# A chunked recurrence in a token mixer: its small matrices as two heads by four chunks of 64x64, on diagonal quarters of the TensorE array

## The chip, the cores and the metric

The kernel runs on one core of a Trainium2 chip. The metric is the device time of one execution in microseconds, as the median of several runs. An engine is one of TensorE (PE in the profile; its weight loads are PEld), VectorE (DVE), ScalarE (ACT), GpSimd (POOL) and SyncE (SP, which here only issues transfers).

## The reference: what is computed

Two transformer blocks on 256 tokens of width 1024, all in fp32. The first block is a SwiGLU feed-forward, a token mixer and another feed-forward, each on a normalised input and added to the residual. The second has two kinds of attention, a dense feed-forward and a mixture of eight experts. Only the token mixer is touched. It projects the input to 3344 columns and splits them in four branches of 256 channels:

```python
y_pool = causal_multiscale_pool(p_pool, ...)                    # windows 2, 4, 8, 16, then a small linear map
o_h    = chunked_gated_linear_attention(q, k, v, log_f)         # 4 heads of 64, "hgrn"
S_t    = S_{t-1} diag(w_t) - (S_{t-1} kk_t)(kk_t * a_t)^T + v_t k_t^T ;  o_t = S_t r_t    # "rwkv", 4 heads of 64
o_g    = chunked_gated_linear_attention(q, k, v, log_a)         # 4 heads of 64, "gla"
y      = concatenate([y_pool, y_hgrn, y_rwkv, y_gla]) ; return y @ w_out
```

The change is about the third branch, the rwkv recurrence over 256 steps, and about the order of the work of the other branches around it.

## The kernel before

**Lanes.** The program is written as one list of steps for each engine (`Lane`); a step waits for the marks given to it and leaves one. The order on an engine is the order in which the Python code emits the steps. Small helpers emit them: `MM` a product (one fp32 product is two instructions in the trace, each with its own weight load), `TT`, `TS`, `STT` elementwise work on VectorE or GpSimd, `AC` an operation of ScalarE. In the trace all steps of a helper have the helper's line, so L1189 is any product of the mixer. ScalarE changes its function table when an operation needs another set of functions; that is an instruction of its own in the trace, ACT_TABLE_LOAD. PSUM has eight banks of 512 columns (`bank[0..7]`).

**Input product.** `linear` multiplies 13 chunks of weights (`MIX_ORDER`) and calls `between` twice for each chunk. Every call advances two generators one step, `left()` (the gla attention, then the preparation `rwkv()`) and `hgrn()` (the hgrn attention). So their work lies between the chunks on each engine. What is left of them is run off behind the last chunk by `zip_longest(*streams)`. `rwkv()` waits there until the last chunk (`held[0]`) is there, then does the small products for decay, rate and gate (L1189 `sb_lora`), with tanh and sigmoid, the square root of the head sums, and a scan over the decays.

**Preparation.** Behind that stands elementwise work on VectorE that makes decayed keys, queries and values (`kkd`, `rd`, `kp`, `bp`, `kc`, `bc_`), and transposes by `to_tokens` (L1196) with copies by ScalarE. `qr` is an operand padded with zeros: four copies spread two heads over it, so that one full 128-row product gives both heads. All this waits for the end of the first attention (`own["done"]`), and the recurrence's products wait for the last copies (`pe.wait(m_kct, m_bct, m_tok, m_g)`).

**Recurrence.** Four heads are two tiles (`ti`) of two heads. The time is cut in four chunks of 64 steps (`RCHUNK`). Inside a chunk the recurrence is a triangular system. `tile_stages(ti)` keeps its matrices as four full 128x128 ones (`probs`: two heads by two blocks of two chunks), of which only the two diagonal 64x64 blocks are not zero. It has these parts, between `yield`s:

- Masks: for each block three score products into `ba`, `bb_`, `bc_`, and seven VectorE operations with 128x128 masks (`akt`, `abt`, `xx`, `invt`, `inv`, `art`, `arbt`).
- Inverse by doubling: for w in 2, 4, 8, 16, 32 a product (`mx`), its copy by ScalarE (`xx`), products with the inverse and its transpose (`mb_`, `ma`), and two additions on VectorE; GpSimd masks the next level's matrix (`ml`).
- Solve: products with the solved values `yy`, then outputs and chunk states in 64x64 products, then a chain over the chunks 1 and 2 and the last products, which end in `outs[ti]`.

`others()` is a third generator: the pool branch (`bands`, `wp`), the norm and gate of the hgrn branch (output part 1) and of the gla branch (output part 3), and the split of each finished branch into a high and a low part (`split`). `zip_longest(tile_stages(0), tile_stages(1), others())` takes the three in turns; that fixes the order on every engine.

**End.** The group mean (a product with `headsum`) starts when both tiles and the gla branch are through. Then `project` multiplies the four branches by `w_out` in the order 0, 1, 3, 2, with `group_norm()` between, whose result is branch 2 and is used last. `ahead` and `fetch` emit the transfer of a weight chunk (SyncE, line 257) and its split into a high part (ScalarE, L263) and a low part (VectorE, L267). The next phase, the second feed-forward, needs the whole result.

## Time and profile before

| | us |
|---|---|
| median of 3 runs | 1711.46 |
| lowest and highest of them | 1709.71 and 1711.62 |
| the profiled execution | 1713.05 |
| its span in the trace | 1711.2 |
| TensorE busy | 1615.1 |
| VectorE busy | 1216.3 |
| ScalarE busy | 871.7 |
| GpSimd busy | 128.2 |

All rows are of the one profiled execution, and times are microseconds from the start of its span. Busy time is what the profiler recorded; matmuls overlap, so their mean duration is longer than their distance. A timeline row gives the start of the first instruction of a merged run, the time to the end of its last one, their count and, in brackets, how long the engine had been idle and what released it. The stage that the change rewrites runs from the end of the input product (330.4) to the group mean (418.07).

### The profile page before, as it was taken

Reading aid. Unit: us, or ns where it says so; the run is one execution under the profiler, and the core shown is the slowest. Engines: PE = TensorE matmul, PEld = TensorE weight load, DVE = VectorE, ACT = ScalarE, POOL = GpSimd, SP = SyncE. Lnnn points to the kernel's source line nnn. Section 1 sums busy time; section 2 is a strip of 40 time slices with the busy share of each in tenths; the row PEclk is TensorE's granted clock in tenths of the full one; section 3 lists DMA queues with packets and bytes.
Section 4 is the critical chain, followed back from the end, with each engine's and each line's share of the span. In section 5 each row is a group of like instructions: output and inputs, shape, how many; then the busy total and the mean of one; then the engine's idle time right before and its main releaser. Section 6 shows DMA issues by size and latency. Waiting matters only on the chain.

```text
span 1711.2 us, 23833 instructions
## 1 busy us (share of the span) xinstructions
PE 1615.1 (94%) x9812; PEld 1391.3 (81%) x9812; DVE 1216.3 (71%) x1447; ACT 871.7 (51%) x1011; POOL 128.2 (7%) x142
## 2 busy tenths in 40 slices
PE   7999989888999998989899999889999999999997
PEld 6999979777899998946799987568877877877875
DVE  5777769754677775444677763557888988988996
ACT  5334456442533344343434342447777777777775
POOL 1000012310000000052000001520000000000000
PEclk9999999989999998999899999998999999999999
DMA  8777633210588764504577760025998988988983
GB/s 307 282 282 263 235 120 130 85 50 26 199 334 300 289 236 146 175 25 162 197 276 264 265 241 1 1 99 225 367 329 315 363 320 309 367 322 325 347 322 131
DMA packets 51918, 386.45 MB, mean 226 GB/s; under 512 B 5888, under 2 KB 6224, under 8 KB 7904
## 3 DMA queue, kind: packets, MB, share of 16 engines
q1 hardware_dynamic: 50400, 376.16, 59.9%
q0 software_dynamic: 1408, 8.73, 1.3%
q8 instruction: 80, 1.31, 0.3%
q14 instruction: 30, 0.25, 0.0%
HBM read 383.82 MB, written 1.05 MB: 225 GB/s over the span
## 4 chain that ended last, share of the span: by engine, by line
PE 79%; DVE 9%; ACT 5%; issue 3%; DMA 2%; POOL 2%; DVEq 0%; ACTq 0%; SPq 0%
PE bank L295 21%; PE bank L297 21%; PE bank L296 20%; PE bank L1189 5%; PE bank L455 2%; DVE sb_wlo L267 2%; ACT sb_whi L263 2%; DMA sb_ada_raw<-in_ada 1%; PE bank L1755 1%; PE bank L1714 1%; DVE sb_ada_acc L600 1%; DVE sb_wlo L2181 1%; PE bank L1910 1%; PE bank L1870 1%; PE bank L610 1%
## 5 line engine op out<-in xcount | busy, mean ns | idle before, releaser
L267 DVE TENSOR_TENSOR sb_wlo<-sb_raw,sb_whi 128x2048 fp32r<-128x2048 f32 x137 | 313.7, 2291 | 191.4 <-ACT sb_whi L263 191.4
L295 PE MATMUL bank<-sb_xhi,sb_whi 128*128 128x256 f32 x1344 | 384.3, 286 | 6.6 <-DVE sb_wlo L267 6.1
L296 PE MATMUL bank<-sb_xlo,sb_whi 128*128 128x256 f32 x1344 | 382.1, 284 | 0.0
L297 PE MATMUL bank<-sb_xhi,sb_wlo 128*128 128x256 f32 x1344 | 382.0, 284 | 0.0
L263 ACT ACTIVATE sb_whi<-sb_raw 128x2048 fp32r<-128x2048 f32 x137 | 261.5, 1909 | 183.6 <-PE bank L297 178.6
L295 PEld LDWEIGHTS bank<-sb_xhi,sb_whi 128*128 128x128 f32 x1344 | 259.7, 193 | 10.7 <-DVE sb_wlo L267 7.0
L296 PEld LDWEIGHTS bank<-sb_xlo,sb_whi 128*128 128x128 f32 x1344 | 259.9, 193 | 1.1
L297 PEld LDWEIGHTS bank<-sb_xhi,sb_wlo 128*128 128x128 f32 x1344 | 259.7, 193 | 0.0
L2181 DVE TENSOR_TENSOR sb_wlo<-sb_raw,sb_whi 128x2048 fp32r<-128x2048 f32 x84 | 191.5, 2286 | 16.2 <-ACT sb_whi L2175 14.6
L295 PE MATMUL bank<-sb_whi,sb_slots_hi 128*128 128x512 f32 x448 | 182.4, 407 | 0.0
L297 PE MATMUL bank<-sb_whi,sb_slots_lo 128*128 128x512 f32 x448 | 176.7, 394 | 0.0
L296 PE MATMUL bank<-sb_wlo,sb_slots_hi 128*128 128x512 f32 x448 | 176.6, 394 | 0.0
L2175 ACT ACTIVATE sb_whi<-sb_raw 128x2048 fp32r<-128x2048 f32 x84 | 160.8, 1916 | 26.9 <-PE bank L297 26.5
L295 PE MATMUL bank<-sb_whi,sb_hhi 128*128 128x512 f32 x368 | 146.4, 398 | 1.1 <-DVE sb_hlo L574 1.1
L297 PE MATMUL bank<-sb_whi,sb_hlo 128*128 128x512 f32 x368 | 144.9, 394 | 0.0
L296 PE MATMUL bank<-sb_wlo,sb_hhi 128*128 128x512 f32 x368 | 144.8, 393 | 0.0
L600 DVE SCALAR_TENSOR_TENSOR sb_ada_acc<-sb_ada_raw,sb_cact,sb_ada_acc 128x384 f32<-128x384 f32 x224 | 138.6, 619 | 6.9
L297 PEld LDWEIGHTS bank<-sb_whi,sb_slots_lo 128*128 128x128 f32 x448 | 84.1, 188 | 20.1
L296 PEld LDWEIGHTS bank<-sb_wlo,sb_slots_hi 128*128 128x128 f32 x448 | 84.6, 189 | 16.5
L295 PEld LDWEIGHTS bank<-sb_whi,sb_slots_hi 128*128 128x128 f32 x448 | 84.3, 188 | 16.4
L295 PEld LDWEIGHTS bank<-sb_whi,sb_hhi 128*128 128x128 f32 x368 | 69.9, 190 | 15.8 <-issue 1.2
L297 PEld LDWEIGHTS bank<-sb_whi,sb_hlo 128*128 128x128 f32 x368 | 69.7, 189 | 15.3
(465 smaller groups left out, 2574.4 us busy)
## 6 DMA issues: line engine op xcount, KB each, us to landing
sb_raw<-in_ffn SPq DMA_DIRECT2D x98, 1024.0 KB, 4.8
sb_raw<-in_moe SPq DMA_DIRECT2D x86, 1024.0 KB, 5.0
sb_ada_raw<-in_ada SPq DMA_DIRECT2D x32, 1536.0 KB, 6.5
sb_cst<-in_moe SPq DMA_DIRECT2D x28, 1024.0 KB, 4.8
sb_xn<-in_moe SPq DMA_DIRECT2D x27, 1024.0 KB, 5.7
sb_ada_raw<-in_moe SPq DMA_DIRECT2D x27, 1024.0 KB, 5.1
sb_raw<-in_w_in SPq DMA_DIRECT2D x13, 1024.0 KB, 4.7
sb_raw<-in_na_qk SPq DMA_DIRECT2D x8, 1024.0 KB, 4.7
```

The lines of the kernel that those rows point to most:

```text
L263: e.activation(whi[s][:, :], raw[s][:, :], ACT.Copy).then_inc(s_hi[s], 1)
L267: e.tensor_tensor(wlo[s][:, :], raw[s][:, :], whi[s][:, :], ALU.subtract).then_inc(s_lo[s], 1)
L295: e.matmul(dst, wh, xh, start=first, stop=False, skip_group_check=skip)
L296: e.matmul(dst, wh, xl, start=False, stop=False, skip_group_check=skip)
L297: return e.matmul(dst, wl, xh, start=False, stop=last, skip_group_check=skip)
L455: l = e.matmul(tile(k)[:, b * P:(b + 1) * P], x[:, b, k * P:(k + 1) * P], diag(b), start=True, stop=True)
L600: l = e.scalar_tensor_tensor(ada_acc[:, :], ada_raw[:, k, :], cact[:, k:k + 1], ada_acc[:, :], ALU.mult, ALU.add)
L610: l = e.matmul(MODP[:, at:at + 1], ada_acc[:, i * P:(i + 1) * P], ones[:, 0:1], start=True, stop=True)
L1189: return pe.step(lambda e: e.matmul(o, l, r, start=start, stop=stop), *after)
L1714: m = pe.step(lambda e, q=q: e.matmul(bk[:, q * T:(q + 1) * T], *scores(i, q), start=mask is None, stop=True), *m_ready(i), m_sread.get(i ...
L2175: e.activation(highs[c % 4][:, :], ring[(c - 2) % NR], ACT.Copy).then_inc(m_hi, 1)
L2181: e.tensor_tensor(lows[c % 4][:, :], ring[(c - 2) % NR], highs[c % 4][:, :], ALU.subtract).then_inc(m_lo, 1)
```

## The change: what it does

- The matrices of the recurrence are kept as [two heads x 64 rows, four chunks x 64 columns]. Every product of `tile_stages` is one of eight 64x64 products (two heads, four chunks), head 0 on rows and columns 0 to 63 of the array and head 1 on 64 to 127. The scores take decayed keys and queries side by side (128 moving columns).
- The masks are 64 wide and repeated; one operation per bank masks both of the matrices in it (`steps`). The two copies into the inverse and its transpose take one operation each for four chunks.
- The zero-padded `qr`, its memset and its four copies go. The transposes are 64x64 products too (`transposed`), with token-by-channel results for one chunk each.
- Those of the gate-weighted operands (`kc`, `bc_`), the copies, the gate product (`g2`), the bonus and the value product (`z`) move into `others()`, behind the score products. They use one bank, `b_o`, one after another.
- `streams` is `[hgrn(), left()]`. `rwkv()` goes on when chunk 4 is there, one before the last; its square root stands before tanh. The two sigmoid-like gates are computed at other places, and `e1` and `to_end` are computed before the end of the first attention.
- In `others()` high and low parts are split by a step, the pool's scale and bias are applied by ScalarE, a square root with no other use stands in the first step, and the generator ends two steps later. The high and low parts of `w_out[3]` are emitted in `group_norm()`.

```diff
-    same = s // RCHUNK == t // RCHUNK
-    main["before"] = same & (s < t)
-    main["upto"] = same & (s <= t)
-    main["after"] = same & (s > t)
+    r, u = np.arange(P)[:, None] % RCHUNK, np.arange(RCHUNK)[None, :]
+    main["steps"] = np.concatenate([r < u, r <= u], axis=1)
+    main["eyes"] = r == u
     for m in (1, 2, 4, 8, 16, 32, 64):
-        pair = (s // (2 * m) == t // (2 * m)) & (s // m % 2 == 0) & (t // m % 2 == 1)
-        main[f"level{m}"] = pair
+        main[f"level{m}"] = (s // (2 * m) == t // (2 * m)) & (s // m % 2 == 0) & (t // m % 2 == 1)
         if m < RCHUNK:
-            main[f"levelT{m}"] = pair.T
+            main[f"inner{m}"] = (r // (2 * m) == u // (2 * m)) & (r // m % 2 == 0) & (u // m % 2 == 1)
+    main["inner1T"] = (r // 2 == u // 2) & (r % 2 == 1) & (u % 2 == 0)
+    main["rest"] = np.zeros((P, P))
...
+            while 4 not in held:
                 yield
-            pe.wait(*held.values(), *w_lora)
...
-            m5 = AC(xg, xg, ACT.Sigmoid, held[8])
+            lent["xg"] = AC(xg, xg, ACT.Sigmoid, held[8])
+            (s_w, _, _), (s_a, _, _) = env["split_ahead"]
+            b_w, b_a = bank[4 + s_w], bank[4 + s_a]
+            lent["banks"] = b_w, b_a, bank[4 + 3 - s_w - s_a]
+            pe.wait(held[12], held[4], *w_lora)
...
+                m6 = MM(b_w[:, i * T:(i + 1) * T], lora[:, 0, i * P:(i + 1) * P], lo_in, True, True, m4)
             for i in range(GT):
...
+            own["gate_ready"] = AC(hg, hg, ACT.Sigmoid, held[4])
+            lent["decays"], lent["rates"] = m6, m7
...
+            m1 = TT(dve, e1, cum[:, :, :], gate[:, :, :], ALU.subtract, mc, lent["done"])
...
+            lent["to_end"] = TT(dve, g4, end, c4, ALU.subtract, m1)
+            lent["e1"] = AC(e1, e1, ACT.Exp, m1)
...
-        streams = [left(), hgrn()]
...
+        streams = [hgrn(), left()]
...
-        for _ in zip_longest(*streams):
-            pass
+        for z in (streams[0], streams[0], streams[1], streams[0]):
+            next(z, None)
...
+            def transposed(dst, src, *after):
+
+                for i in range(GT):
+                    for c in range(NCH):
+                        for hh, hs in enumerate(halves):
+                            m = MM(dst[hs, i * T + c * HD:i * T + (c + 1) * HD], src[hs, i, chunk(c)],
+                                   ident[hs, hh * HD:(hh + 1) * HD], True, True, *after)
+                return m
...
+            mt_v = transposed(b_w, v, held[7], lent["decays"])
+            for l in (act, dve):
+                l.wait(own["done"])
+            m_em = AC(em, cum[:, :, :], ACT.Exp, lent["scanned"], scale=-1.0)
...
-            mkd = TT(dve, kkd, bb[:, :, :], e1, ALU.mult, m_e1, mkk)
+            mkd = TT(dve, kkd, bb[:, :, :], e1, ALU.mult, lent["e1"], mkk)
...
+            mbp = TT(dve, bp, bb[:, :, :], em, ALU.mult, m_em, mb)
+            mt_kk = transposed(bank[3], kkd, mkd, lent["roots"])
+            m_yy = [AC(eights(homes[ti][2])[:, 0:8:2, :], bank[3][:, ti * T:(ti + 1) * T].rearrange("p (c v) -> p c v", v=HD),
+                       ACT.Copy, mt_kk) for ti in range(GT)]
+            m_vt = AC(vt, blocks(b_w[:, :]), ACT.Copy, mt_v)
...
-                    rhs = qr[:, ti, :, :, ts].rearrange("p a h t -> p (a h) t")
-                    m1 = MM(ba[:, :], kp[:, ti, ts], rhs, True, True, free[0], mkp, mqr)
-                    m2 = MM(bb_[:, :], bp[:, ti, ts], rhs, True, True, free[1], mbp)
-                    for hh in range(2):
-                        m3 = MM(bc_[:, hh * P:(hh + 1) * P], qr[:, ti, 0, hh, ts], bp[:, ti, ts], True, True, free[2])
-                    of = lambda z: z[:, blk:4:NB, :]
-                    m_akt = TT(dve, of(akt), n4(ba)[:, 0:2], many(C("before"), 2), ALU.mult, m1)
-                    m_abt = TT(dve, of(abt), n4(bb_)[:, 0:2], many(C("before"), 2), ALU.mult, m2)
-                    ml = TT(dve, of(xx), n4(bb_)[:, 0:2], many(C("level2"), 2), ALU.mult, m2)
-                    m_it, m_i = (dve.step(lambda e, to=of(z), mask=level(name), src=n4(b)[:, 0:2]:
-                                          e.copy_predicated(to, mask, src), *m_pre[ti], m3)
-                                 for z, name, b in ((invt, "level1", bb_), (inv, "levelT1", bc_)))
-                    f0 = TT(dve, of(art), n4(ba)[:, 2:4], many(C("upto"), 2), ALU.mult, m1)
-                    f1 = TT(dve, of(arbt), n4(bb_)[:, 2:4], many(C("upto"), 2), ALU.mult, m2)
...
+                ba, bb_, bc_ = (bank[0], bank[1], bank[2]) if ti == 0 else (bank[3], b_w, b_a)
+                free = (own["done"], mkk) if ti == 0 else (m_yy[-1], m_vt, lent["rates"])
...
+                def each(dst, width, lhs, rhs, *after, close=True):
+                    for c in range(NCH):
+                        for hs in halves:
+                            m = MM(dst[hs, c * width:(c + 1) * width], lhs(c, hs), rhs(c, hs), True, close, *after)
+                    return m
+
+                both = lambda c, hs: qr[hs, :, ti, chunk(c)]
+                m1 = each(bb_, 2 * HD, lambda c, hs: bp[hs, ti, chunk(c)], both, mbp, mkd, mrd, *free)
+                m2 = each(bc_, HD, lambda c, hs: kkd[hs, ti, chunk(c)], lambda c, hs: bp[hs, ti, chunk(c)])
+                m3 = each(ba, 2 * HD, lambda c, hs: kp[hs, ti, chunk(c)], both, mkp)
+                steps = C("steps").rearrange("p (o q t) -> p o q t", o=1, q=2).broadcast_to([P, NCH, 2, HD])
+                quads = lambda z: z.rearrange("p (c q) t -> p c q t", q=2)
+                level = lambda name: many(C(name), NCH)
+                m_i, m_it = (dve.step(lambda e, to=to, mask=level(name).bitcast(U32), src=src:
+                                      e.copy_predicated(to, mask, src), m_pre[ti], m2)
+                             for to, name, src in ((inv, "inner1T", n4(bc_)), (invt, "inner1", n8(bb_)[:, 0:8:2, :])))
+                ml = TT(dve, lv, n8(bb_)[:, 0:8:2, :], level("inner2"), ALU.mult, m1)
+                m_abt = TT(dve, quads(ab), quads(n8(bb_)), steps, ALU.mult, m1)
+                m_akt = TT(dve, quads(ak), quads(n8(ba)), steps, ALU.mult, m3)
...
+                    mx = each(ba, HD, lambda c, hs: lv[hs, c, :], lambda c, hs: inv[hs, c, :], ml, m_i, m_akt)
...
+                        ml = TT(pool, lv, abt, level(f"inner{2 * w}"), ALU.mult, mx, m_abt)
                     mx = AC(xx, n4(ba), ACT.Copy, mx)
...
+                        ma = each(bb_, HD, lambda c, hs: invt[hs, c, :], lambda c, hs: xx[hs, c, :], mx, m_it, m_abt)
                         m_i = TT(dve, inv, inv, n4(bb_), ALU.add, ma)
-                    m_it = TT(dve, invt, invt, n4(bc_), ALU.add, mb_, m_i)
+                    mb_ = each(bc_, HD, lambda c, hs: xx[hs, c, :], lambda c, hs: invt[hs, c, :], mx, m_it)
+                    m_it = TT(dve, invt, invt, n4(bc_), ALU.add, mb_)
...
+                pair = lambda c: slice(2 * c, 2 * c + 2)
+                my = each(ba, 2 * HD, lambda c, hs: invt[hs, c, :], lambda c, hs: yy[hs, pair(c), :], outs["z"], m_it)
+                my = AC(yy, n8(ba), ACT.Copy, my)
                 yield
 
-                for n, (hh, blk) in enumerate(probs):
...
+                mq_ = each(bb_, HD, lambda c, hs: yy[hs, 2 * c, :], lambda c, hs: arbt[hs, c, :], my)
+                for c in range(NCH):
...
+                        mo_ = MM(bc_[hs, chunk(c)], vt[hs, ti, c, :], art[hs, c, :], False, True)
+                mqq = TT(dve, qq, n4(bb_), rd[:, ti, :].rearrange("p (c t) -> p c t", t=RCHUNK), ALU.add, mq_)
...
+                for c in range(NCH - 1):
+                    for hs in halves:
+                        o1 = ba[hs, c * HD:(c + 1) * HD]
+                        o2 = ba[hs, (NCH + c) * HD:(NCH + c + 1) * HD]
+                        MM(o1, yy[hs, 2 * c, :], bct[hs, ti, c, :], True, True, outs["bc"])
+                        MM(o2, kct[hs, ti, c, :], vt[hs, ti, c, :], True, False, outs["kc"])
+                        m2 = MM(o2, bct[hs, ti, c, :], yy[hs, 2 * c + 1, :], False, True)
...
+                for i in range(GT):
+                    m8 = MM(b_o[:, i * T:(i + 1) * T], g2[:, i * P:(i + 1) * P], rw[:, 7, :], True, True,
...
+                mkc = TT(dve, kc, k, gate[:, :, :], ALU.mult, m_ge, mk, mkd)
+                mbc = TT(dve, bc_, bb[:, :, :], gate[:, :, :], ALU.mult, m_ge, mb)
+                lent["gate_ready"] = AC(gg, gg, ACT.Silu, held[12])
+                m_table = AC(heads[:, 1, 0:1], env["epss"][:, 0:1], ACT.Sqrt)
...
+                    m_bon = MM(b_o[:, i * T:(i + 1) * T], C("headsum"), tmp[:, i, :], True, True, m2, m)
+                outs["bonus"] = m = TT(dve, r, b_o[:, :].rearrange("p (k t) -> p k t", k=2), v, ALU.mult, m_bon, mrd, mt_v)
...
+                m = transposed(b_o, kc, mkc, m)
+                outs["kc"] = m = AC(kct, blocks(b_o[:, :]), ACT.Copy, m)
...
+                m = transposed(b_o, bc_, mbc, m)
+                outs["bc"] = m = AC(bct, blocks(b_o[:, :]), ACT.Copy, m)
...
+                            mz = MM(b_o[hs, ti * T + c * HD:ti * T + (c + 1) * HD], akt[hs, c, :], vt[hs, ti, c, :],
+                                    True, True, laid[ti], m_vt, m)
...
+                    m = AC(p[:, i, :], b_o[:, i * T:(i + 1) * T], ACT.Identity, m1, m_rest,
+                           scale=V("pool_scale", i), bias=scaled_bias[:, i:i + 1])
...
-                split(3, gq, m)
+                mh = high(3, gq, m)
...
-                env["ahead"](w_out[3])
+                low(3, gq, mh)
...
+                        ALU.mult, ALU.add, outs["mean"])
                 m = AC(tmp[:, :, :], oo[:, :, :], ACT.Square, m)
+                env["ahead"](w_out[3])
```

## Rows read from the trace of the kernel before

**Rows 1.** The page: busy time by engine, the chain that ended last, two groups of instructions.

```profile
PE 1615.1 (94%) x9812; PEld 1391.3 (81%) x9812; DVE 1216.3 (71%) x1447; ACT 871.7 (51%) x1011; POOL 128.2 (7%) x142
...
PE 79%; DVE 9%; ACT 5%; issue 3%; DMA 2%; POOL 2%; DVEq 0%; ACTq 0%; SPq 0%
...
L267 DVE TENSOR_TENSOR sb_wlo<-sb_raw,sb_whi 128x2048 fp32r<-128x2048 f32 x137 | 313.7, 2291 | 191.4 <-ACT sb_whi L263 191.4
...
L263 ACT ACTIVATE sb_whi<-sb_raw 128x2048 fp32r<-128x2048 f32 x137 | 261.5, 1909 | 183.6 <-PE bank L297 178.6
```

**Rows 2.** Windows by stage: length, busy us of each engine, granted clock, DMA share, GB/s.

```profile
core 0: us, PE busy (x) PEld busy (x) DVE busy (x) ACT busy (x) POOL busy (x), PEclk, DMA share, GB/s
330.40:339.00 8.60, 6.24 (x53) 4.82 (x52) 5.79 (x10) 6.34 (x11) 4.04 (x3) 1.00 0.27 92
339.00:352.40 13.40, 6.87 (x37) 5.37 (x37) 10.59 (x18) 8.91 (x16) 3.64 (x5) 0.67 0.00 0
352.40:366.00 13.60, 13.04 (x49) 7.89 (x49) 9.64 (x28) 4.11 (x5) 0.00 (x0) 0.82 0.00 0
366.00:404.00 38.00, 33.58 (x282) 32.03 (x281) 18.37 (x31) 12.80 (x21) 10.44 (x8) 0.96 0.15 57
404.00:414.40 10.40, 10.23 (x140) 9.43 (x140) 5.42 (x10) 2.44 (x5) 0.00 (x0) 1.00 0.30 102
```

**Rows 3.** Timeline of TensorE: start, us, instruction, count, idle before and releaser.

```profile
330.44 1.16 PE L1189 MATMUL bank<-sb_qd,sb_ex 64*128 64x128 f32 x16
...
336.73 1.57 PE L1189 MATMUL bank<-sb_sc,sb_tok 128*64 128x256 f32 x16 [1.67 <-DVE sb_sc L1281]
...
352.38 3.75 PE L1189 MATMUL bank<-sb_xn,sb_p 128*128 128x512 f32 x4 [0.73 <-ACT sb_p L1186]
...
371.32 1.06 PE L1189 MATMUL bank<-sb_rstd,sb_late_y 128*128 128x128 f32 x8
...
377.76 1.06 PE L1189 MATMUL bank<-sb_rstd,sb_late_y 128*128 128x128 f32 x8
...
391.17 3.60 PE L1189 MATMUL bank<-sb_own 128*128 128x128 f32 x16 [2.73 <-ACT sb_own L1186]
...
404.05 1.16 PE L1189 MATMUL bank<-sb_ada_raw,sb_own 128*128 128x128 f32 x8 [1.73 <-DVE sb_own L1170]
...
408.11 0.38 PE L1189 MATMUL bank<-sb_ada_raw,sb_tok 128*64 128x128 f32 x2
408.42 0.33 PE L1189 MATMUL bank<-sb_p,sb_ada_raw 64*64 64x64 f32 x2
...
415.49 0.46 PE L1189 MATMUL bank<-sb_p 64*64 64x64 f32 x8 [0.91 <-DVE sb_p L1580]
416.17 1.25 PE L1189 MATMUL bank<-sb_p 64*64 64x64 f32 x28 [0.22 <-DVE sb_p L1170]
...
418.07 1.10 PE L1189 MATMUL bank<-sb_oo,sb_cst 128*128 128x256 f32 x4 [0.65 <-DVE sb_oo L1170]
```

**Rows 4.** Timeline of ScalarE around the end of the first attention.

```profile
329.38 0.63 ACT L1186 ACTIVATE sb_ex<-sb_ex 128x512 f32<-128x512 f32 x1 [1.92 <-DVE sb_ex L1170]
...
331.04 0.41 ACT L1186 ACTIVATE sb_p<-sb_p 64x256 f32<-64x256 f32 x1
331.46 1.28 ACT L1186 ACT_TABLE_LOAD   x1
...
333.08 0.96 ACT L1186 ACTIVATE sb_rcum<-bank,sb_vec 128x256 f32<-128x256 f32 x2
...
338.37 0.60 ACT L1186 ACTIVATE sb_p<-bank 128x512 f32<-128x512 f32 x1 [1.96 <-PE bank L1189]
```

**Rows 5.** Timeline of VectorE: scans, preparation, a mask, an addition.

```profile
334.76 1.27 DVE L1391 TENSOR_TENSOR_SCAN sb_rcum<-sb_cst,sb_gate 128x256 f32<-128x256 f32 x2
...
340.34 1.14 DVE L1175 TENSOR_SCALAR sb_tmp<-sb_rwkv_a,sb_vec,sb_rest 128x256 f32<-128x256 f32 x2
...
361.60 0.41 DVE L1170 TENSOR_TENSOR sb_own<-bank,sb_cst 128x256 f32<-128x256 f32 x1
...
371.52 0.69 DVE L1170 TENSOR_TENSOR sb_ada_raw<-sb_ada_raw,bank 128x512 f32<-128x512 f32 x1 [5.86 <-PE bank L1189]
```

More of the change, by code:

```diff
@@ L1625, in others @@
                 yield
+                low(0, pooled, mh)
+                for blk in range(NB):
+                    for i in range(GT):
+                        ms = MM(b_o[:, blk:blk + 1], tmp[:, i, blk * P:(blk + 1) * P], ones[:, 0:1],
+                                i == 0, i == GT - 1, m1, m)
+                m = AC(heads[:, 1, 0:NB], b_o[:, 0:NB], ACT.Sqrt, ms, m_table, bias=env["epss"][:, 0:1], scale=1.0 / G)
+                m2 = AC(gate[:, :, :], gq, ACT.Square, mbc, mkc)
+                yield
```

278 lines of the change are left out of this document (105 added, 173 removed).

## The prediction

> **What bounds the kernel now.** The page comes first [rows 1]: TensorE is busy for 94% of the span, and 79% of the chain that ended last is its work. The phases of the program follow each other (feed-forward, mixer, feed-forward, ...), each consuming what the one before left, so a mixer that ends earlier moves everything behind it forward by as much, if no weight transfer becomes late. The windows by stage come second [rows 2]. The last input product ends at 330.4 and the output product starts behind the group mean at 418.07 [rows 3]; that stretch is what the change rewrites. The DMA share in it is 0.00 to 0.30, so transfers don't set it. Its stages have different limits:
> - 330.4 to 339: ScalarE, 6.34 of 8.6 us, through its table loads [rows 2, 4].
> - 339 to 352.4: VectorE, 10.59 of 13.4 us. TensorE works half the time, its granted clock is 0.67, and the first score product waits for all transposes and their copies.
> - 352.4 to 366: the first half is TensorE at a low clock (four 512-column instructions take 3.75 us), the rest VectorE: 28 operations, 9.64 us.
> - 366 to 404: TensorE, 33.58 of 38 us. This is the inverse by doubling, five levels for two tiles. A level takes 6.44 us (371.32 to 377.76 [rows 3]).
> - 404 to 418: TensorE again until 414.4, then a chain of small steps.
>
> **The change part by part.** The zero point is the start of the group mean, 418.07. At the full clock an instruction of a 128x128 product goes every 0.112 us ((1.06-0.275)/7, 371.32). A 64-row half with 128 columns, alternating between halves, goes every 0.059 ((1.16-0.272)/15, 330.44). A 64x64 quarter goes every 0.034 to 0.038 (415.49 and 416.17); there the two heads already lie on diagonal quarters [rows 3]. Two instructions make one fp32 product. So eight quarter products (16 instructions, 0.54 us) replace four full ones (8 instructions, 0.89 us). For quarters with 128 moving columns I take 0.059, their nearest row; the ends are 0.056 (half of 0.112) and 0.112.
>
> *Up to the end of the first attention.* The square root of the head sums now stands ahead of tanh and sigmoid, and the attention's last collection stands behind the scans and two more VectorE operations. ScalarE: the exponential ends at 330.01; three table loads of 1.28 (root, tanh, sigmoid) with 0.2, 0.41 and 0.42 of work between them, and 0.96 for the decay sigmoids, end at 335.85. Before, these sigmoids ended at 334.04, after a single load [rows 4]. VectorE then has the scans (1.27), three operations of about 0.66 (0.69 each at 371.52) and two copies of half their width (0.41 each, back to back 0.35), to 339.75 [rows 5]. The product (1.57, 336.73 [rows 3]) and the copy end at 342.0, against 338.97: **+3.0 us**. Bounds: +0.3 if the root costs no switch, +3.5. *The Trainium skill, "ScalarE: Activation LUTs", section "What ACT_TABLE_LOAD costs", gives about 2.66 us for each switch, drain included; by it the two added switches would be 2.8 us dearer. Here a load and the 0.4 us operation behind it were over 1.62 us after the load's start (331.46 to 333.08 [rows 4]).*
>
> *Preparation.* The zero-filled operand and its four copies go, and all transposes but two, with the gate-weighted operands, move behind the first score products. What the scores wait for on VectorE is the pair at 340.34 (1.14) and seven operations of 0.69 [rows 5]: 6.0, say 6.15 beside a busy GpSimd. It was 13.41 (338.97 to 352.38): **-7.25**. Bounds: -6.5 and -8.
>
> *Masks.* A tile needs 16+16 instructions with 128 columns and 16 with 64: 2.43 us at the full clock. The first tile meets the half clock, as the same place does now (0.82 over the stage [rows 2]), so 4.86+2.43. Behind them the gate product takes 4 instructions of 256 columns, 0.215 each (1.10 for four with the last one's tail, 418.07 [rows 3]). That is 8.15 against 13.6: **-5.45**. The 28 masked operations of 0.34 become 10, some 4.6 us, under the products. Bounds: clock full, 2.4 less; both tiles at half, 2.4 more.
>
> *Inverse.* It was 38.06 (to 404.05). ScalarE first has the gate copy, two table loads and their functions ahead of the first evacuation: 0.65+1.28+0.63+1.28+0.2+0.4+0.15 = 4.6 us from the first product to the second, and here TensorE waits 2.5. Then 26 groups of 16 quarter instructions: 14.1. Three moved sets of 32 quarter instructions (two transposes, one value product): 3.3. Bands 1.4 (the same 16 shapes as 336.73, without the tail), pool 0.86, sums 8x0.1, spread 4x0.112: 3.5. A stall of 0.6 where four ScalarE operations of the pool stand ahead of an evacuation. For starting groups and for changing between full products and quarters I add 3.5: a change takes 0.31 from start to start for two instructions that otherwise take 0.11 (408.11 to 408.42 [rows 3]), twelve of them are 2.4, and 0.05 for each other group. Sum 29.65: **-8.4**. GpSimd's masks halve to 0.65 and stay hidden (8 took 10.44 [rows 2]); uncovered they would cost 0.65 a tile and level. VectorE's additions fall from 0.69 to 0.41 [rows 5]. Bounds: quarters at 0.028 and free changes, 7 less; quarters at 0.038, 2 more; waits in every level, 3 more.
>
> *Values and states.* From the solve (404.05) to the end of the second tile's products it was 10.35. Now the normalised first branch stands on VectorE and ScalarE ahead of the solved values' copy: 3.35 instead of 2.0; then 84 quarter instructions a tile at 0.036 are 6.0 instead of 8.35: **-1.0**, by one either way.
>
> *End.* From there to the mean it was 3.7. The last branch's head spread (16x0.059) and its four VectorE operations (two of 0.41, two of 0.69, a wait for ScalarE between) now lie between the small steps: **+2.25**, by one either way.
>
> *Output product.* The split of the third output weight (ScalarE 1.91, VectorE 2.29 [rows 1]) moves into the group norm. It ends some 7 us behind the mean and is used 13 us behind it, under products that last some 23 us; its transfer needs only the band products, long done: 0. Uncovered it would be 4.2. One more row of constants and the smaller constant block: 0.
>
> Sum: 3.0-7.25-5.45-8.4-1.0+2.25 = -16.85. The profiled execution took 1713.05 (span 1711.2) and would take 1696.2. Its time lies 1.6 above the median of the runs, 1711.46, so I forecast **1694.6**.
>
> **Rivals.**
> *A. Everything overlaps better.* Quarters at 0.028, half of the 0.056 that 64 columns would take alone, the clock up early, changes free: 10 less, but the waits then show, so 1687. For it: the row at 330.44 is near perfect overlap. Against it: 415.49 shows 0.034.
> *B. Waits take the place of the products.* One tile's level is product 0.73, evacuation 0.4, product 0.73, addition 0.41, with 0.3 between them: 2.6 us against 3.3 of TensorE for both tiles. If the others' work on ScalarE and VectorE pushes this chain so far that the tiles stop overlapping, a level is twice 2.6 and a piece of other work, and the inverse gives nothing: 1703. For it: 391.17 and 404.05, where TensorE waited 2.73 and 1.73 behind just such work.
> *C. The heads don't overlap.* Both heads of a group now write one bank. If they take turns there, a quarter costs 0.056 with 64 columns and 0.112 with 128: 0.02x750+0.053x96 = 20 more, 1714.6: no difference. Against it: in 415.49 both heads of a tile write one bank, at 0.034. *The Trainium skill, "TensorEngine Tiling (Array Packing)", section "Restrictions and Gotchas", says that different row tiles cannot access the same PSUM bank simultaneously: by that rule C is what happens. The row at 415.49 speaks against it.*
> *D. Slower: the clock.* TensorE's clock falls to 1.2 GHz and stays there, because it does less work between waits. Now it is granted 0.50 to 0.67 around 339 to 357, where TensorE works in pieces, and one wait of 2.73 us is followed by 16 instructions in 3.60 instead of 1.95 us (391.17). At half clock the 750 quarter instructions, 96 wider ones and the full products behind the masks cost up to 36 us more: 1731. It decides from 17/36, 47% of the stretch, at the low clock. Against it: 404 to 418, the part with the most quarters and with waits, is granted 1.00 [rows 2].
>
> **How the numbers follow.** About 0.2% (3.4 us) is what a measurement can tell from no change. Chances: forecast 0.58, A 0.18, B 0.13, C 0.05, D 0.06. Faster 0.89, same 0.05 (C), slower 0.06 (D). The bounds of the parts don't all fall on one side; taken together they give 8 to either side. The range reaches to most of A and to B: 1684 to 1703. What it leaves out is C, D and tails of 0.08.
>
> **What would show it.** Start of the mean near 401. The first attention ends near 342 and the first score product starts near 348; if it starts before 346, the root's switch was hidden. Masks: 10 VectorE operations. A level without other work near 3.3 to 4 us; 5 or more is C or D, which the granted clock and the spacing of quarter instructions (0.034 or 0.056) tell apart. A TensorE wait of some 2.5 us behind ScalarE in the first level. A granted clock under 0.8 from 360 to 395 would make me wrong, and so would a late weight in the output product. If it comes out far under 1687, I counted waits that don't add.

## The result, and the profile after

The changed kernel takes 1682.0 us in the median (1678.82 to 1687.45, four runs) where the kernel before, on the same chip, takes 1710.6: the ratio is 0.984, with an interval of 0.981 to 0.987. On a second chip it was 1684.6 against 1708.0, ratio 0.985 (0.983 to 0.987). So it is faster by 23 to 29 us; 17 were forecast, and the first median lies 2 us below the forecast range of 1684 to 1703 (the second is just inside it). The profiled execution took 1684.34 (span 1682.5), 28.7 us less than that of before.

The page first, in the same lines as [rows 1]:

```profile
PE 1592.5 (95%) x10292; PEld 1374.0 (82%) x10292; DVE 1204.4 (72%) x1426; ACT 867.6 (52%) x1010; POOL 116.4 (7%) x138
...
PE 80%; DVE 9%; ACT 5%; issue 3%; POOL 2%; DMA 1%; DVEq 0%; ACTq 0%; SPq 0%
...
L267 DVE TENSOR_TENSOR sb_wlo<-sb_raw,sb_whi 128x2048 fp32r<-128x2048 f32 x137 | 314.1, 2293 | 193.9 <-ACT sb_whi L263 193.7
```

TensorE has 480 more instructions and is busy 22.6 us less; GpSimd has 12 us less. The rest of the program is as it was: the largest VectorE group has the same mean and nearly the same idle time. The windows of the rewritten stretch, cut where the work changes (columns as in [rows 2]):

```profile
core 0: us, PE busy (x) PEld busy (x) DVE busy (x) ACT busy (x) POOL busy (x), PEclk, DMA share, GB/s
331.00:337.40 6.40, 3.60 (x16) 2.52 (x14) 3.78 (x8) 5.29 (x10) 0.00 (x0) 0.77 0.24 101
337.40:341.00 3.60, 3.58 (x31) 2.94 (x32) 0.26 (x3) 1.12 (x3) 0.00 (x0) 0.58 0.00 0
341.00:346.30 5.30, 2.53 (x70) 2.08 (x66) 5.20 (x9) 2.81 (x6) 0.00 (x0) 1.00 0.01 3
346.30:352.00 5.70, 5.63 (x100) 5.08 (x100) 3.95 (x11) 0.00 (x0) 0.00 (x0) 1.00 0.00 0
352.00:356.40 4.40, 2.50 (x37) 1.80 (x36) 4.16 (x6) 4.23 (x7) 1.60 (x2) 1.00 0.02 6
356.40:377.10 20.70, 19.99 (x544) 18.68 (x544) 7.93 (x19) 8.23 (x21) 4.26 (x6) 1.00 0.41 155
377.10:385.40 8.30, 8.11 (x208) 7.83 (x208) 4.34 (x12) 2.53 (x6) 0.00 (x0) 1.00 0.01 2
385.40:391.30 5.90, 2.91 (x59) 2.31 (x57) 4.43 (x14) 0.63 (x1) 0.00 (x0) 1.00 0.01 4
```

The reader is to see two things. From 341 to 391 the granted clock is 1.00 (2.4 GHz), where [rows 2] had 0.67, 0.82 and 0.96. And the long window of the inverse, 20.7 us with 544 instructions, is 97% TensorE. The starts that bound the stages are in TensorE's timeline (to be held against [rows 3]):

```profile
330.42 3.53 PE L1191 MATMUL bank<-sb_p,sb_lora 128*128 128x256 f32 x8 [2.95 <-ACT sb_p L1188]
...
337.42 2.88 PE L1191 MATMUL bank<-sb_sc,sb_tok 128*64 128x256 f32 x16 [2.83 <-DVE sb_sc L1283]
...
346.37 1.09 PE L1191 MATMUL bank<-sb_xn,sb_p 64*64 64x128 f32 x16 [1.39 <-DVE sb_p L1172]
...
352.01 0.68 PE L1191 MATMUL bank<-sb_ada_raw 64*64 64x64 f32 x16
...
356.49 1.15 PE L1191 MATMUL bank<-sb_ada_raw 64*64 64x64 f32 x32 [1.49 <-ACT sb_ada_raw L1188]
357.48 0.63 PE L1191 MATMUL bank<-sb_rcum,sb_rstd 64*64 64x64 f32 x16
357.94 0.63 PE L1191 MATMUL bank<-sb_rstd,sb_rcum 64*64 64x64 f32 x16
358.41 1.10 PE L1191 MATMUL bank<-sb_cst,sb_xn 64*64 64x64 f32 x32
...
365.06 1.56 PE L1191 MATMUL bank<-sb_raw,sb_p 128*64 128x256 f32 x16
...
371.31 1.05 PE L1191 MATMUL bank<-sb_cst,sb_tmp 128*128 128x1 f32 x8 [0.55 <-ACT sb_tmp L1188]
...
377.12 1.09 PE L1191 MATMUL bank<-sb_ada_raw 64*64 64x128 f32 x16
...
388.40 0.46 PE L1191 MATMUL bank<-sb_p 64*64 64x64 f32 x8 [1.48 <-DVE sb_p L1172]
...
391.28 1.72 PE L1191 MATMUL bank<-sb_oo,sb_cst 128*128 128x256 f32 x4 [0.58 <-DVE sb_oo L1172]
392.44 0.99 PE L295 MATMUL bank<-sb_whi,sb_xhi 128*128 128x512 f32 x1
```

The copy of the first attention's output, on ScalarE, ends at 340.97 where it ended at 338.97 before [rows 4]:

```profile
340.37 0.60 ACT L1188 ACTIVATE sb_p<-bank 128x512 f32<-128x512 f32 x1 [2.45 <-PE bank L1191]
```

The mean starts at 391.28, 26.8 us earlier than at 418.07 [rows 3]. The 1.9 us that the spans differ by beyond that lie in the rest of the program and are less than executions of one kernel differ among themselves. Part by part, forecast and measured:

| part | forecast | measured, from to | difference |
|---|---|---|---|
| stages ahead of 330 (not costed) | 0 | -2.95 (the last attention exponential starts at 326.43 for 329.38) | -2.95 |
| to the copy of the first attention's output | +3.0 | +4.95 (with the line above +2.0: 338.97 to 340.97) | +1.95 |
| preparation, to the first score product | -7.25 | 13.4 to 5.4: -8.0 | -0.75 |
| masks, to the inverse's first product | -5.45 | 13.6 to 5.64: -8.0 | -2.5 |
| inverse, to the solve | -8.4 | 38.06 to 25.1: -12.95 | -4.55 |
| values and states | -1.0 | 10.35 to 8.3: -2.05 | -1.05 |
| end, to the mean | +2.25 | 3.67 to 5.85: +2.2 | -0.05 |
| sum | -16.85 | -26.8 | -9.95 |

This is one execution. In run 9, the same kernel once more, the stretch from that exponential to the mean took 66.4 us where the table's took 64.85 and the kernel before 88.7, so some 1.6 of the ten are how one execution differs from another.

Three of the missing ten come from a place that the prediction never looked at. The two kernels already differ at 244 us, where `streams` has its new order. ScalarE and then TensorE of the kernel before:

```profile
245.93 0.20 ACT L1186 ACTIVATE sb_lbs<-sb_lbs 128x2 f32<-128x2 f32 x1 [1.63 <-DVE sb_lbs L1170]
246.04 1.89 ACT L263 ACTIVATE sb_whi<-sb_raw 128x2048 fp32r<-128x2048 f32 x1
...
248.56 2.08 PE L1189 MATMUL bank<-sb_p 64*128 64x128 f32 x16 [3.87 <-ACT sb_p L1166]
```

The same of the changed kernel:

```profile
244.28 0.20 ACT L1188 ACTIVATE sb_lbs<-sb_lbs 128x2 f32<-128x2 f32 x1
244.39 1.90 ACT L263 ACTIVATE sb_whi<-sb_raw 128x2048 fp32r<-128x2048 f32 x1
...
246.91 1.16 PE L1191 MATMUL bank<-sb_p 64*128 64x128 f32 x16 [2.25 <-ACT sb_p L1168]
```

Before, a 0.2 us exponential of the gla branch stood on ScalarE ahead of the copy that TensorE needed and waited 1.63 us for VectorE. With hgrn emitted first its operand is ready. TensorE's wait is 2.25 in place of 3.87, and the half-array products behind it take 1.16 us in place of 2.08 (the granted clock over them is 1.00, against 0.50, 1.2 GHz). The copy of a later chunk comes at 257.42 instead of 260.37.

### The profile page after: what moved, and what is told of

It is laid out like the page before. It is cut to its first block, busy times and chain, and to the rows that moved or that the text cites. A ratio compares the mean times of both kernels' runs of the same rounds, so it can differ in the third digit from the quotient of the medians.

```text
span 1682.5 us, 24758 instructions
## 1 busy us (share of the span) xinstructions
PE 1592.5 (95%) x10292; PEld 1374.0 (82%) x10292; DVE 1204.4 (72%) x1426; ACT 867.6 (52%) x1010; POOL 116.4 (7%) x138
## 3 DMA queue, kind: packets, MB, share of 16 engines
HBM read 383.63 MB, written 1.05 MB: 229 GB/s over the span
## 4 chain that ended last, share of the span: by engine, by line
PE 80%; DVE 9%; ACT 5%; issue 3%; POOL 2%; DMA 1%; DVEq 0%; ACTq 0%; SPq 0%
PE bank L295 22%; PE bank L297 21%; PE bank L296 21%; PE bank L1191 4%; ACT sb_whi L263 2%; PE bank L455 2%; DVE sb_wlo L267 2%; PE bank L1765 1%; PE bank L1724 1%; PE bank L1920 1%; DVE sb_wlo L2191 1%; PE bank L610 1%; PE bank L1880 1%; ACT sb_whi L2185 1%; POOL sb_h L1747 1%
```

## The experiments

The kernel before was run beside them in each series: 1710.1 us (17 runs) for the first four, 1707.5 (9) for the next four, 1708.0 (9) for the last two. Where a sentence says "than the changed kernel", it compares ratios (0.984 and 0.985 in its two series) or traces.

**1. The order of the streams alone, in the kernel before.**

```diff
-        streams = [left(), hgrn()]
+        streams = [hgrn(), left()]
```

> The kernel before with one line of the change: the two attention streams advance in the order hgrn, left instead of left, hgrn. Theory (order): the trace of the changed kernel is 2.95 us ahead at the copy of chunk 7 of the input product (257.42 against 260.37) before any quarter product has run, because a tiny exponential on ScalarE (sb_lbs) no longer waits 1.63 us for VectorE, the copy behind it and TensorE's wait shrink (3.87 to 2.25 us) and the clock is not lowered as long behind it. The copies of the chunks from the fourth on come about 2.9 us earlier here too, and the run is 2 to 4 us shorter than before. Rival (the preparation does it): no gain, within 1 us of before, and TensorE's wait near 244.4 stays at 3.9 us.

Measured: 1707.0 (12 runs), ratio 0.9985 (0.9976 to 0.9994), 2.6 us by the ratio and 3.2 by the medians. As expected. Its trace has the wait of 2.25 before the half-array products and their 1.16 us. So the uncosted 2.95 is the emission order and nothing else of the change; it is a gain of its own.

**2. The changed kernel with the order of before.** The next steps are drawn from the same generators in the same order.

```diff
-        streams = [hgrn(), left()]
+        streams = [left(), hgrn()]
...
-        for z in (streams[0], streams[0], streams[1], streams[0]):
+        for z in (streams[1], streams[1], streams[0], streams[1]):
```

> The changed kernel with the streams back in the order left, hgrn, all else kept. Theory (order): TensorE's wait near 244.4 is 3.9 us again, the copies from the fourth on are 2.9 us later, and the run is 2 to 4 us longer than the changed kernel's 1682.0, so 1684 to 1686, a gain on before of 24.5 to 26.5. Rival: no difference to the changed kernel, or a loss of over 5 us because the order matters more where the preparation has moved forward.

Measured: 1689.2 (1683.7 to 1690.2), ratio 0.9876 (0.9859 to 0.9892): 4 to 6.5 us slower than the changed kernel, more than the 2 to 4 that were expected. In its trace the 3.87 wait is back, the last product of the first attention is 5.1 late (342.50) and the mean 5.7 (396.97). The order is worth more here than the 3 us in the kernel before, and ScalarE's timeline says why:

```profile
334.43 1.28 ACT L1188 ACT_TABLE_LOAD   x1
335.73 0.63 ACT L1188 ACTIVATE sb_ex<-sb_ex 128x512 f32<-128x512 f32 x1
```

This exponential belongs to the first attention. With hgrn emitted first it runs at 326.43; here it stands behind the root, the tanh and the sigmoids and behind a load of its own, and the attention's last two products come behind waits of 4.58 and 3.06 us. The 0.6 between 5.1 and 5.7 is an idle stretch of TensorE that run 3 shows better.

**3. The square root behind the sigmoids.**

```diff
-            lent["roots"] = AC(heads[:, 0, :], bank[3][:, 0:NB * MH], ACT.Sqrt, m_sum)
...
             own["gate_ready"] = AC(hg, hg, ACT.Sigmoid, held[4])
+            lent["roots"] = AC(heads[:, 0, :], bank[3][:, 0:NB * MH], ACT.Sqrt, m_sum)
```

> The changed kernel with the square root of the head sums back behind the sigmoids (my term for the end of the first attention). Theory: two of the five table loads between the last attention exponential and the next exponential lie on the path; without root, load, tanh comes at 327.1 instead of 329.86, TensorE's wait before the small products (2.95 us) goes, the half clock at 337.4 to 340.4 goes with it, and the first attention ends 2.9 to 4.5 us earlier: 1677.5 to 1679 for 1682.0. Rival: the last collection waits for the score product behind it and for the scans in any case, so that under 1 us comes out.

Measured: 1677.9 (1676.4 to 1679.0), ratio 0.9814 (0.9800 to 0.9827), 4 to 7 us faster than the changed kernel. ScalarE of the changed kernel, then of this one:

```profile
326.43 0.63 ACT L1188 ACTIVATE sb_ex<-sb_ex 128x512 f32<-128x512 f32 x1 [1.91 <-DVE sb_ex L1172]
327.08 1.28 ACT L1188 ACT_TABLE_LOAD   x1
328.37 0.18 ACT L1188 ACTIVATE sb_heads<-bank 128x8 f32<-128x8 f32 x1
328.57 1.28 ACT L1188 ACT_TABLE_LOAD   x1
329.86 0.42 ACT L1188 ACTIVATE sb_p<-sb_p 64x256 f32<-64x256 f32 x1
330.29 1.28 ACT L1188 ACT_TABLE_LOAD   x1
```

```profile
325.80 0.63 ACT L1188 ACTIVATE sb_ex<-sb_ex 128x512 f32<-128x512 f32 x1 [1.92 <-DVE sb_ex L1172]
326.34 0.40 ACT L1188 ACTIVATE sb_p<-sb_p 64x256 f32<-64x256 f32 x1
326.76 1.28 ACT L1188 ACT_TABLE_LOAD   x1
328.05 0.42 ACT L1188 ACTIVATE sb_p<-sb_p 128x256 f32<-128x256 f32 x1
```

The time is as expected. The tanh (64x256) needs no load behind the exponential. The root between the two puts itself and two loads ahead of it: the tanh starts 3.43 us behind the exponential's start instead of 0.54, and TensorE's `sb_lora` products, which wait for it, start at 326.88 instead of 330.42. The first attention's last product, the first score product and the bonus are all 3.44 earlier. Of that, 0.63 was there already at the exponential, so the place of the root is worth 2.8 against this profile of the changed kernel, and 2.2 against that of run 9 (8.18 us from the exponential to the last product, against 10.99 and 10.39). The mean is only 0.5 earlier in this one execution. From the second product of the inverse to the pool's it took 1.5 us longer: TensorE was granted 0.72 between 352 and 358, where the changed kernel had 1.00. And 1.4 were lost where TensorE stood still in the middle of a group:

```profile
374.21 0.56 PE L1191 MATMUL bank<-sb_rstd,sb_rcum 64*64 64x64 f32 x12 [1.19 <-issue]
```

"issue" means that it waited for nothing that the profile shows. The same gap is in the same group in the profiles of runs 2 (0.40), 6 (0.61), 7 (0.82) and 10 (1.21), and not in the two of the changed kernel; no run looked for its cause. So the start of the mean in one trace doesn't settle a difference of a microsecond or two.

**4. Each group head by head, instead of the heads in turns.**

```diff
-                    for c in range(NCH):
-                        for hs in halves:
+                    for hs in halves:
+                        for c in range(NCH):
```

> The changed kernel with the eight quarter products of a group emitted head by head (four chunks of head 0, then four of head 1) instead of in turns; the same products, instructions, banks and waits. Theory (overlap): 16 instructions take 0.463 us in the changed kernel because neighbours lie on different diagonal quarters; in this order they share a quarter, each costs 0.056 and a group 0.85 or more. 32 groups with 64 columns and 6 with 128 then cost 32x0.4+6x0.9 = 18 us more: near 1700. Rival (issue): the 0.029 us per instruction is what a small instruction costs, and the array's quarters don't matter: within 2 us of 1682.0. Rival (bank): both heads take turns at the bank already, also within 2 us.

Measured: 1692.2 (1689.2 to 1693.9), ratio 0.9898 (0.9881 to 0.9915), some 8 to 10 us slower than the changed kernel. Neither number was met. The reason stands in TensorE's timeline:

```profile
361.89 0.56 PE L1191 MATMUL bank<-sb_ada_raw 64*64 64x64 f32 x10
362.25 0.27 PE L1191 MATMUL bank<-sb_rstd,sb_rcum 64*64 64x64 f32 x1
362.30 0.22 PE L1191 MATMUL bank<-sb_ada_raw 64*64 64x64 f32 x1
362.35 0.22 PE L1191 MATMUL bank<-sb_rstd,sb_rcum 64*64 64x64 f32 x1
...
362.47 0.56 PE L1191 MATMUL bank<-sb_rstd,sb_rcum 64*64 64x64 f32 x10
```

At each change of head some three instructions of the one lie between three of the other (362.25 to 362.42). A group takes 0.58 us (361.89 to 362.47), 0.036 for an instruction, against 0.465 (357.48 to 357.94) in turns, and not the 0.9 of instructions that never overlap. An estimate from these rows: with two changes a group, six of its 16 instructions are hidden, and ten times 0.056 is 0.56. So the two diagonal quarters do work at the same time, and an order without turns finds three quarters of the overlap in this row, at the seams. Consecutive groups write different banks; that it also holds within one bank is shown by the 0.029 in turns, where both heads write the same one. A part of the rest is clock: 0.64 from 356.9 to 360.6, where the changed kernel had 1.00.

**5. SiLU and the root's table load ahead of the second product.**

```diff
+            lent["gate_ready"] = AC(gg, gg, ACT.Silu, held[12])
+            m_table = AC(heads[:, 1, 0:1], env["epss"][:, 0:1], ACT.Sqrt)
...
-                lent["gate_ready"] = AC(gg, gg, ACT.Silu, held[12])
-                m_table = AC(heads[:, 1, 0:1], env["epss"][:, 0:1], ACT.Sqrt)
```

> The changed kernel with the silu of the last gate and the otherwise unused square root emitted behind the copy of the transposed values, where ScalarE idles for 5.9 us before the gate copy at 352.12, instead of behind the gate copy. Theory (the stall I put into the first level is real): in the changed kernel TensorE waits 1.49 us at 356.49 for the first evacuation, with two table loads ahead of it on ScalarE. That wait goes except for what the bonus product needs (about 354 to 355): 1 to 1.5 us less, and the clock cannot fall behind it, as it does in some executions: 1680 to 1681 for 1682.0, and a smaller spread. Rival: VectorE's bonus operands (353.88) hold TensorE at the same place, nothing is gained.

Measured: 1683.5 (1678.4 to 1687.3), ratio 0.9862 (0.9838 to 0.9886): no gain that a median shows, and no smaller spread (8.9 us); neither was as expected. The trace has the mechanism, though. TensorE in this kernel, to be held against 356.49 above:

```profile
355.48 1.13 PE L1191 MATMUL bank<-sb_tmp,sb_cst 128*128 128x256 f32 x4 [0.49 <-DVE sb_tmp L1180]
356.54 1.15 PE L1191 MATMUL bank<-sb_ada_raw 64*64 64x64 f32 x32
```

The wait of 1.49 behind ScalarE is gone: 1.06 from the bonus to the next product instead of 2.61. In this execution the score products ran at a clock of 0.72 and had given the 1.6 us away before that (6.21 us for the two tiles' instead of 4.58).

**6. The masked operations by block: 28 in place of 10.**

```diff
...
-                ml = TT(dve, lv, n8(bb_)[:, 0:8:2, :], level("inner2"), ALU.mult, m1)
-                m_abt = TT(dve, quads(ab), quads(n8(bb_)), steps, ALU.mult, m1)
-                m_akt = TT(dve, quads(ak), quads(n8(ba)), steps, ALU.mult, m3)
+                for b in (slice(0, 2), slice(2, 4)):
...
+                    ml = TT(dve, lv[:, b, :], n8(bb_)[:, 0:8:2, :][:, b, :], level("inner2")[:, b, :], ALU.mult, m1)
+                    for q in range(2):
+                        m_abt = TT(dve, quads(ab)[:, b, q], quads(n8(bb_))[:, b, q], steps[:, b, q], ALU.mult, m1)
+                for b in (slice(0, 2), slice(2, 4)):
+                    for q in range(2):
+                        m_akt = TT(dve, quads(ak)[:, b, q], quads(n8(ba))[:, b, q], steps[:, b, q], ALU.mult, m3)
```

> The changed kernel with its 10 masked VectorE operations cut into 28 smaller ones (each again for two chunks and one matrix), as many as before the change; the same elements, masks and results. Theory (the masks lie under the products now): the second tile's masks end 1 to 1.5 us later, and that is all: 1683 to 1683.5. Rival (the merged masks carry the 8 us that this stage got shorter): 5 us or more, 1687 and up.

Measured: 1680.6 (1679.1 to 1687.0), ratio 0.9859 (0.9836 to 0.9883): no loss that a median shows, less than was expected. In the trace the bonus starts 0.7 later, but the second product of the inverse is where it was (10.12 us behind the first score product in both). The mean is 0.97 later, and 0.86 of that arise between 371.40 and 378.07, where this profile has the gap of run 3 (0.61, "issue"). So one operation per bank is worth nothing that these runs can tell. From 346.3 to 352 TensorE is busy for 5.63 of 5.70 us and VectorE for 3.95: the stage that was VectorE's before (28 operations, 9.64 us, [rows 2]) is TensorE's now, and it is not the count of masked operations that made it so. How the 8 us that the stage got shorter divide between the shorter products, their clock and the preparation that left the queues, no run shows.

**7. The moved preparation put back: four steps of the others ahead of the score products.**

```diff
-            for _ in zip_longest(tile_stages(0), tile_stages(1), others()):
+            rest_of = others()
+            for _ in range(4):
+                next(rest_of)
...
+            for _ in zip_longest(tile_stages(0), tile_stages(1), later()):
```

(`later()` yields four times and then goes on with `rest_of`.)

> The changed kernel with the first four steps of the other branches (gate product, bonus, both transposes of the gate-weighted operands with their copies) emitted ahead of the score products again, in the turns that follow nothing takes their place. Theory: the first score product starts about 7 us later than 346.4, the preparation's whole gain; but the first levels lose 3.9 us of moved products and the 1.5 us wait behind the table loads, so the run is only 1.5 to 2.5 us longer: 1683.5 to 1684.5. Moving work behind the scores then bought 2 us net of the 8 that the preparation got shorter. Rival: the levels don't get shorter, since evacuations and not products set them: 7 us longer, 1689.

Measured: 1685.3 (1679.9 to 1687.7), ratio 0.9868 (0.9844 to 0.9891), 2.4 to 5 us slower than the changed kernel by the ratios, whose intervals touch; 1.5 to 2.5 were expected. The score products start 14.57 us behind the first attention's product instead of 8.95, so 5.6 later. From that product to the mean it takes 56.25, against 53.86 and, in run 9, 56.04 in the changed kernel, and 1.1 of the 56.25 lie where this profile has the gap of run 3 (0.82). So at the mean 0.2 to 2.4 of the 5.6 are left: what is moved behind the score products isn't free, and more than half of it comes back in the stages that it fills.

**8 and 10. The root late and the tables early together, twice. 9. The changed kernel beside it.**

> The changed kernel with the root behind the sigmoids and with the two table loads early, together. In the profile of the run with the root late alone, the first attention ended 3.44 us earlier, but 2.9 us of that were lost again: the clock fell to 0.66 behind the wait for the table loads (352 to 358). Theory: without that wait the clock stays up and both gains add: 1676 to 1677, the fastest so far. Rival: the clock falls at another place, 1678 or more.

Measured: 1675.4 (1673.7 to 1679.0), ratio 0.9817 (0.9797 to 0.9837), about as expected (1676 to 1677).

> The changed kernel unaltered, once more, on the same chip as the next run. Both theories of the prediction's failure: a time of 1679 to 1687 us, some 26 to 30 below the kernel before; the group mean's first product at 391 to 393 us of the span. If single executions differ because TensorE's clock falls behind other waits from time to time, the stages that were at 1.00 in the first profile (346.3 to 391.3) can be at half clock for a few us here, and the mean then starts 1 to 3 us later without any other row of the stage changing.

Measured: 1684.6 (1679.8 to 1686.7), ratio 0.9854 (0.9834 to 0.9873); mean at 391.50. The time and the mean are as expected, the distance to the kernel before (23.4 us) is less than the 26 to 30. Two windows that were at 1.00 in the first profile stand at 0.84 and 0.81 here:

```profile
352.00:356.40 4.40, 2.92 (x46) 2.46 (x48) 2.78 (x5) 2.70 (x6) 0.45 (x1) 0.84 0.00 0
...
385.40:391.30 5.90, 3.11 (x54) 2.47 (x50) 4.12 (x14) 0.63 (x1) 0.00 (x0) 0.81 0.00 1
```

> The square root of the first attention behind its sigmoids, and the SiLU with the root's next table load ahead of the inverse's second product, once more, beside the changed kernel on one chip. Theory (the two table places cost 3.4 and 1.6 us, and they add): 5 us below the changed kernel's median of this call, 1674 to 1678 us, and the mean's first product about 5 us earlier. Rival (the lead of this version over the changed kernel came from a clock that happened to stay high in its executions): less than 2 us between the two medians.

Measured: 1677.4 (1672.8 to 1683.7), ratio 0.9824 (0.9798 to 0.985). The difference of the two medians of this series is 7.2 us (5 by the ratios, whose intervals touch), and the mean's first product is 3.4 earlier than in run 9 (388.07) although this profile has low stretches and a gap of 1.21 us; about 5 was expected. In run 8, whose clock was 1.00 from 345 to 400, it was 4.9 earlier than in the first profile of the changed kernel. By the ratios of runs 8 and 10 the two table places are worth 2.4 to 6.3 us together. But the root's place alone (run 3, 0.9814) has as low a ratio as both (0.9817 and 0.9824): what the second place adds, the 1.6 us of its wait, shows in the traces and in no median. These versions are the fastest that were run, by 1.8% under the kernel before. The timeline of run 10 shows both: the `sb_lora` products follow without a wait, and the second product follows the bonus.

```profile
326.95 1.97 PE L1191 MATMUL bank<-sb_p,sb_lora 128*128 128x256 f32 x8
...
350.50 1.13 PE L1191 MATMUL bank<-sb_tmp,sb_cst 128*128 128x256 f32 x4 [0.49 <-DVE sb_tmp L1180]
351.57 1.15 PE L1191 MATMUL bank<-sb_ada_raw 64*64 64x64 f32 x32
```

## Why the prediction was wrong

The direction, the mechanism and the order of the terms were right; the sum was 10 us too small, and the likeliest case should have been beyond its own rival A (1687). The four steps below are 11.7 us together; what goes the other way is the first attention (1.95) and the products of the other branches in the inverse (0.7); the rest are differences under 1 us. By its steps:

**Quarters (wrong, some 3.7 us).** The step "a 64x64 quarter goes every 0.034 to 0.038" was read from rows of 8 and 28 instructions in the closing chain, where every group starts behind a wait and feeds another. The inverse runs at 0.029 (0.465 for 16, 357.48 to 357.94), half of the 0.056 that 64 columns cost alone (half of the prediction's 0.112 for 128; run 4 fits it). The row of 8 is no different now: 388.40 takes the same 0.46. It was a true row of the wrong place. Of the 512 quarters from 356.49 to 377.12 it cost 2.5 us too much (17.4 for 14.9), of the 168 in values and states (at 0.036) another 1.2.

**Starts and changes of shape (wrong, 2.5).** "For starting groups and for changing I add 3.5." From 356.49 to 377.12 there are 20.63 us; 512 quarters are 14.9, the products of the other branches 4.2 (365.06 to 366.54 and three like it), the one wait 0.55. That leaves 1.0 for all starts and changes. The 4.2 were forecast at 3.5, so up to 0.7 of what changes cost may be counted in there. The price came from one row, 408.11 to 408.42 [rows 3], multiplied by twelve.

**Clock in the masks (wrong, 2.5).** "The first tile meets the half clock, as the same place does now." It met 1.00. The price of a clock was carried from one execution of the kernel before into a stage whose work ahead was new. The 96 score instructions met 1.00 in eight of the ten profiles of the changed kernel and its variants, and 0.72 and 0.77 in runs 5 and 4. Run 5 has the same work and the same wait (1.39) ahead of them as the changed kernel, so what decides isn't shown; the likelier value was the full clock.

**The order of the streams (missing, 2.95).** The diff had the line and the prediction's sum did not. Run 1 gives it 2.6 to 3.2 alone.

**First attention (too small by 1.95, outside its upper bound of +3.5).** ScalarE's part was nearly right: from the end of the exponential to that of the decay sigmoids it took 6.4 us (327.06 to 333.48) where 5.84 were forecast and 4.03 were taken before [rows 4]; the 0.5 between is a wait for the `sb_lora` product. Run 3 puts the root's place at 2.2 to 2.8. The mis-sized step is "the product (1.57) and the copy": they took 3.55 instead of 2.24, because the product met the half clock (0.58) behind a longer wait, 2.83 against 1.67. Those 1.3 us were no term and in no bound. (In run 9 the part is +4.34 instead of +4.95.) *By the price in the Trainium skill, "ScalarE: Activation LUTs", section "What ACT_TABLE_LOAD costs", each switch would be 2.66 us: the trace doesn't agree, a load and its function go from 328.57 to 330.29, in 1.72 us.*

**Right.** The preparation (-8.0 for -7.25, on its lower bound), the 4.6 us from the first to the second product (4.48, though TensorE waited 1.49 behind ScalarE and 0.48 behind VectorE, and not the 2.5 of the forecast), and the end (+2.2 for +2.25). The masks lie under the products as said (run 6). The output product took no late weight.

**The rivals.** A is nearest. Most of its "10 less" came (3.7, 2.5 and 2.5 from the three steps that it names), its "but the waits then show" did not; its argument against itself was the row at 415.49. B fell: a level is six groups of 0.465, 2.8 us, which is more than the 2.6 of its chain and its products lie under each other's evacuations; TensorE is 97% busy, and only 0.55 us of waits lie in the whole inverse behind the second product. C fell by the spacing of 0.029 with both heads in one bank; run 4 shows the overlap, and what it is worth (8 to 10 us), from the other side. *By the rule in the Trainium skill, "TensorEngine Tiling (Array Packing)", section "Restrictions and Gotchas", different row tiles cannot access the same bank simultaneously; a spacing below the 0.056 of one quarter alone doesn't agree with it here.* D fell: the clock is 1.00 from 341 to 391.3, and where the inverse of another run met a lower one it was for some us only (0.72 over 6 us in run 3, 0.64 over 3.7 in run 4).

What stays open: which executions get the low clock, and which the gap without a releaser. The same kernel had 1.00 and 0.84 in the same window in two profiles. And of the difference between the two series of the changed kernel (28.6 and 23.4 us under before) nothing is explained beyond that.

## What to carry to other kernels

A price for a repeated instruction is to be read from start to start inside a long unbroken run of its kind, or the nearest shape halved; short groups in a chain of waits gave 0.034 to 0.038 here for 0.029. Every line of a diff that touches the order of emission gets a term, also if it lies 80 us ahead of the change: a 0.2 us operation that waits at the head of a queue cost 3 us. A table function on ScalarE is cheapest next to others of its table, and one move of it was worth 4 to 7 us here, where a threefold cut of the masked operations was worth nothing that shows. And the start of one stage in one trace isn't the worth of a change: two profiles of one kernel differed by 1.6 us over this stretch.

## What the runs showed of the hardware

- Two heads on diagonal quarters that write one bank run at 0.029 us an instruction (64x64, 64 columns) when they alternate, and at 0.036 when each head's eight come in a row (run 4), where some three instructions overlap at each change of head. With 128 columns, 16 took 0.93 (346.37 to 347.30) before other shapes followed: 0.058.
- In five of ten profiles of the changed kernel and its variants TensorE stood still for 0.40 to 1.21 us inside a group of the inverse, with no releaser that the profile shows (run 3).
- Table loads: an exponential followed by a tanh had none between them (325.80, 326.34 in run 3), a root between them brought two.
- In the changed kernel the granted clock was 0.56 from 330.4 to 334, behind a wait of 2.95 us, 0.58 from 337.4 to 341, behind one of 2.83, and 0.64 from 391.3 to 396, behind waits of 1.48, 0.93 and 0.58; behind 1.46 and 1.39 (343.84 and 346.37) it was 1.00. In run 9 the products behind the first of these waits (2.96) took 1.97 us instead of 3.53. At the end of the stretch the mean's four instructions take 1.72 instead of 1.10 [rows 3] and the first of the output product 0.99 instead of the 0.39 that the same shape takes 4 us later. Whether a stretch gets it differs between executions of one kernel (run 9); nine executions of the changed kernel spread over 8.6 us, and the clock is a part of that, how much was not measured.
